# A two-block network on one core: decay rows of the state-space part by DMA, head pairs in column halves, group products in PSUM, differences on GpSimd

## What is computed

```python
def _ssd(xh, dt, a, bm, cm):                  # 32 heads of 64, 4 groups of 8 heads, state 128
    x = (xh * dt[..., None])...
    a_cs = jnp.cumsum(dt * a, axis=2)
    seg = a_cs[:, :, :, None] - a_cs[:, :, None, :]
    lmat = jnp.exp(jnp.where(causal, seg, -jnp.inf))
    cb = jnp.einsum('bclgn,bcsgn->bclsg', cc, bc)
    y_diag = jnp.einsum('bclsgr,bcsgrp->bclgrp', cb[..., None] * lmat, x)
    ...                                       # plus what earlier chunks pass on
y = _ssd(xh, dt, a, bm, cm) + d_skip[:, None] * xh
```

## Time and profile before

| what | value |
|---|---|
| median of 3 runs | 3531.86 us (3529.06 to 3532.5) |
| the profiled execution, own time | 3530.74 us |
| its span | 3529.1 us |
| PE busy | 2966.5 us, 84% of the span |
| DVE, ACT, POOL busy | 892.6, 701.1 and 153.8 us |
| bytes read from memory | 567.76 MB |
| chain that ended last, by engine | PE 69%, DMA 22%, DVE 3%, ACT 3% |

### The profile page before, as it was taken

The page is one execution under the profiler, slowest core; times in us unless marked ns, Lnnn a source line. Parts: engine busy times, 40 slices in busy tenths (PEclk is TensorE's granted clock), DMA queues, the critical chain, the costliest instruction groups (busy, mean ns, idle before and its releaser), DMA issues.

```text
span 3529.1 us, 39001 instructions
## 1 busy us (share of the span) xinstructions
PE 2966.5 (84%) x14533; PEld 1462.5 (41%) x14534; DVE 892.6 (25%) x1741; ACT 701.1 (20%) x1221; POOL 153.8 (4%) x262
## 2 busy tenths in 40 slices
PE   5999999999984766666666664998899999988999
PEld 3445544344434222222222222554654436455444
DVE  1335659800122000000000003311440114025211
ACT  2113301200111111111111111213641012155310
POOL 1000000000000000000000000000130000002100
PEclk9999999999995989888888887999999999998999
DMA  7251012222223899999999993222002122200020
GB/s 196 96 187 52 1 48 72 71 72 72 72 74 148 333 425 425 424 424 424 424 425 425 424 390 122 70 86 72 1 1 71 48 97 98 79 28 1 25 81 38
DMA packets 125332, 584.16 MB, mean 166 GB/s; under 512 B 15844, under 2 KB 26692, under 8 KB 100660
## 3 DMA queue, kind: packets, MB, share of 16 engines
q1 hardware_dynamic: 107232, 558.06, 39.6%
q0 software_dynamic: 12080, 17.36, 1.9%
q10 hardware_dynamic: 5924, 7.41, 0.6%
HBM read 567.76 MB, written 14.94 MB: 165 GB/s over the span
## 4 chain that ended last, share of the span: by engine, by line
PE 69%; DMA 22%; DVE 3%; ACT 3%; issue 1%; SPq 0%; ACTq 0%; POOL 0%; DVEq 0%; POOLq 0%
PE PS L1508 63%; DMA S<-in_w 19%; PE PS L727 4%; PE PS L935 1%; DMA S<-in_x 1%; DMA ring<-in_w_in 1%; DMA S<-sorted_rows 1%; ACT TAIL L1123 0%; ACT TAIL L1121 0%; ACT TAIL L1119 0%; SPq L293 0%; DVE RSTD L1952 0%; DVE S L2106 0%; ACT L1130 0%; PE PS L395 0%
## 5 line engine op out<-in xcount | busy, mean ns | idle before, releaser
L1508 PE MATMUL PS<-nT,ring 128*128 128x512 f32 x2432 | 1071.5, 600 | 25.0 <-DVE nT L1956 10.3
L1508 PEld LDWEIGHTS PS<-nT,ring 128*128 128x128 f32 x2432 | 466.4, 193 | 608.5 <-issue 597.5
L1508 PE MATMUL PS<-S 128*32 128x256 f32 (+5 forms) x3344 | 366.9, 549 | 137.5 <-DMA S<-in_w 116.4
L1508 PE MATMUL PS<-ring,S 128*32 128x256 f32 (+1 forms) x3360 | 335.9, 555 | 164.3 <-DMA ring<-in_w 137.5
L1508 PE MATMUL PS<-S,ring 128*128 128x512 f32 x896 | 386.2, 592 | 2.5 <-DVE S L1392 1.7
L1508 PEld LDWEIGHTS PS<-ring,S 128*32 128x32 f32 x3360 | 133.4, 127 | 332.8 <-issue 318.4
L1508 PEld LDWEIGHTS PS<-S 128*32 128x32 f32 (+2 forms) x3344 | 138.1, 133 | 315.7 <-issue 268.9
L1508 PEld LDWEIGHTS PS<-S,ring 128*128 128x128 f32 x896 | 170.0, 190 | 216.6 <-issue 216.6
L570 DVE TENSOR_TENSOR S<-S,PS 128x128 f32<-128x128 f32 x65 | 18.7, 287 | 720.6 <-ACT S L487 720.6
L2106 DVE SCALAR_TENSOR_TENSOR S<-S,COL 128x512 f32<-128x512 f32 x240 | 161.0, 744 | 0.1
L487 ACT ACTIVATE S<-PS 128x128 f32<-128x128 f32 x65 | 18.0, 277 | 544.2 <-PE PS L1508 544.2
(11 more groups left out here) (325 smaller groups left out, 2297.6 us busy)
## 6 DMA issues: line engine op xcount, KB each, us to landing
ring<-in_w SPq DMA_DIRECT2D x96, 2048.0 KB, 21.5
S<-in_w SPq DMA_DIRECT2D x96, 2048.0 KB, 21.6
ring<-in_w_in SPq DMA_DIRECT2D x40, 2048.0 KB, 7.8
ring<-in_w_ada SPq DMA_DIRECT2D x12, 2048.0 KB, 11.9
expert_rows<-S POOLq DMA_DIRECT2D x65, 128.0 KB, 10.4
ring<-in_w_ssm_out SPq DMA_DIRECT2D x4, 2048.0 KB, 7.7
ring<-in_cmp_w SPq DMA_DIRECT2D x4, 2048.0 KB, 8.3
ring<-in_w_out SPq DMA_DIRECT2D x4, 2048.0 KB, 7.9
```

Source lines behind the costliest of these rows:

```text
L1508: return pe.matmul(o, l, r, start=start, stop=stop)
```

## The change

- The rows of `RR` are written once to a tensor in device memory (`decay_rows`, 32 x 1280) by a DMA on GpSimd's queue. SyncE then issues one DMA per head that reads one row of it and writes it to all 128 partitions of a buffer of `EB`: 5 KB read 128 times, 640 KB written.
- `EB` has five buffers in place of two, where `CB` and part of `RR` were. The row of head h may be issued once the pair that used its buffer is through on PE: rows 2c+5 and 2c+6 once pair c is.
- GpSimd takes the four differences per head, in place, SBUF to SBUF; ACT's exponentials read and write the same buffer.
- The masked product of a group stays in PSUM (banks 0 to 2 or 3 to 5, in turn by group), masked there by DVE; ACT's copy goes. `masked` multiplies a buffer of `EB` by PSUM.
- PE has no `head_rows`. `pair_y` does two heads in one go and alternates between the halves of the output partitions.
- SyncE's DMAs for heads 0 and 1 stand behind the load of slab GL0, those for heads 2 to 31 between the loads of GL0+2 and GL0+3.

```diff
@@ sync @@
+            def decay_rows(heads):
+                for h in heads:
+                    if h >= NEB:
+                        sp.wait_ge(S("y_mm"), 2 * ((h - NEB) // 2 + 1))
+                    elif h >= 2:
+                        sp.wait_ge(S("xbc_done"), KX)
+                    else:
+                        sp.wait_ge(S("rr_stored"), 16)
+                    sp.dma_start(EB[:, head_buffer(h), :], rr_d[h:h + 1, :].to_broadcast([P, PACK])) \
+                        .then_inc(S(f"row{head_buffer(h)}_landed"), 16)
...
+                if i == GL0 + 1:
+                    decay_rows(range(2))
+                if i == GL0 + NSLOT:
+                    decay_rows(range(2, HEADS))
@@ gpsimd @@
+            pool.wait_ge(S("scalar_milestone"), AFTER["cums_copied"] + 2)
+            pool.dma_start(rr_d, RR[0:HEADS, :]).then_inc(S("rr_stored"), 16)
+            for h in range(HEADS):
+                row_landed(pool, h)
+                for i in range(NT):
+                    pool.tensor_scalar(EB[:, head_buffer(h), P * i:P * i + P], EB[:, head_buffer(h), P * i:P * i + P],
+                                       LS[:, 32 * i + h:32 * i + h + 1], 0.0, ALU.subtract, ALU.min) \
+                        .then_inc(S("diag_exponent"), 1)
@@ tensor @@
+            def pair_y(c):
+                pe.wait_ge(S("m_ready"), 2 * c + 2)
+                if c >= 2:
+                    pe.wait_ge(S("y_out"), c - 1)
                 for i in range(NT):
-                    x_ = XD[:, i, HD * h:HD * h + HD]
-                    m = mm(o[:, P * i:P * i + P], x_, E_[:, P * i:P * i + P], i == 0, i == NT - 1)
+                    for e in range(2):
+                        h = 2 * c + e
+                        o = PS[64 * e:64 * e + 64, 6 + c % 2, :]
+                        m = mm(o[:, P * i:P * i + P], XD[:, i, HD * h:HD * h + HD],
+                               EB[:, head_buffer(h), P * i:P * i + P], i == 0, i == NT - 1)
...
+            group_cb(0)
+            group_cb(1)
+            for c in range(KI):
+                pair_y(c)
+                if c % 4 == 3 and c < 8:
+                    group_cb(c // 4 + 2)
@@ scalar @@
+                row_landed(act, h)
                 for i in (0, 2, 1):
...
+                act.wait_ge(S("diag_exponent"), NT * (h + 1))
+                act.activation(E_[:, 0:512], E_[:, 0:512], ACT.Exp).then_inc(S("e_ready"), 1)
@@ vector @@
+                dve.tensor_tensor(E_, E_, PSF[:, b:b + PACK], ALU.mult).then_inc(S("m_ready"), 1)
```

More of the change, by code:

```diff
@@ L128, in build @@
         S2, S3 = TAIL[:, 0:4096], TAIL[:, 4096:8192]
-        CB, RR = TAIL[:, 8192:9472], TAIL[:, 9472:10752]
+        RR = TAIL[:, 9472:10752]
         X0 = v3(S0[:, 0:4096], D)
@@ L138, in build, with head_buffer @@
         BC = v3(S2, T)
-        EB = v3(TAIL[:, 4096:4096 + 2 * PACK], PACK)
+        NEB = 5
+        EB = v3(TAIL[:, 4096:4096 + NEB * PACK], PACK)
+        def head_buffer(h):
+            return (h + 3) % NEB
         ZS = v3(TAIL[:, 0:1024], T)
@@ L219, in build @@
         sorted_d = nc.dram_tensor("sorted_rows", [NASG, D], F32).ap()
+        rr_d = nc.dram_tensor("decay_rows", [HEADS, PACK], F32).ap()
         y_d = nc.dram_tensor("expert_rows", [NASG + WIN, D], F32).ap()
@@ L1433, in dve_second, with row_landed @@
                 dve.tensor_copy(OUTB[:, n // 2, 512 * (n % 2):512 * (n % 2) + 512], PS[:, n % 4, :]).then_inc(S("out_rows"), 1)
+        def row_landed(eng, h):
+            eng.wait_ge(S(f"row{head_buffer(h)}_landed"), 16 * (h // NEB + 1))
         block = ctx.enter_context(nc.Block())
@@ L1618, in _, with group_cb @@
             ada_columns(11, 2 * 512 + 4 * (11 - ADA0))
-            def group_cb(g, r):
+            def group_cb(g):
                 pe.wait_ge(S("xbc_done"), KX)
-                if r >= 2:
-                    pe.wait_ge(S("rb_dve"), r - 1)
-                    pe.wait_ge(S("rb_act"), r - 1)
+                if g >= 2:
+                    pe.wait_ge(S("m_ready"), HPG * (g - 1))
                 else:
@@ L1636, in group_cb @@
                                BC[:, 4 + g, P * (i + 1):T], True, True)
[L1637 to L1655, removed]
-                for i in range(NT):
-                    x_ = XD[:, i, HD * h:HD * h + HD]
-                    m = mm(o[:, P * i:P * i + P], x_, E_[:, P * i:P * i + P], i == 0, i == NT - 1)
-                    if i in OFF:
-                        m = mm(o[:, P * (i + 1):T], x_, E_[:, OFF[i]:OFF[i] + OFFW[i]], False, False)
-                m.then_inc(S("y_mm"), 1)
@@ L1663, in _ @@
-            pe.wait_ge(S("scalar_milestone"), AFTER["cums_copied"] + 2)
[L1664 to L1677, removed]
+                m.then_inc(S("cb_product"), 1)
@@ new lines, in pair_y @@
+            def pair_y(c):
+                pe.wait_ge(S("m_ready"), 2 * c + 2)
+                if c >= 2:
+                    pe.wait_ge(S("y_out"), c - 1)
+                for i in range(NT):
+                    for e in range(2):
[3 more added lines that the diff above has]
+                               EB[:, head_buffer(h), P * i:P * i + P], i == 0, i == NT - 1)
+                        if i == NT - 1:
+                            m.then_inc(S("y_mm"), 1)
+                    for e in range(2) if i in OFF else ():
+                        h = 2 * c + e
+                        mm(PS[64 * e:64 * e + 64, 6 + c % 2, P * (i + 1):T], XD[:, i, HD * h:HD * h + HD],
+                           EB[:, head_buffer(h), OFF[i]:OFF[i] + OFFW[i]], False, False)
@@ L1678, in _ @@
+            pe.wait_ge(S("scalar_milestone"), AFTER["cums_copied"] + 2)
+            group_cb(0)
[4 more added lines that the diff above has]
+                    group_cb(c // 4 + 2)
+            pe.wait_ge(S("m_ready"), HEADS)
             pe.wait_ge(S("y_out"), KI)
@@ L1864, in _ @@
                         .then_inc(S("xbc_done"), 1)
-            r = 0
             for h in range(HEADS):
[L1868 to L1882, removed]
-                for i in (0, 2, 1):
[L1884 to L1889, removed]
+                E_ = EB[:, head_buffer(h), :]
+                row_landed(act, h)
+                for i in (0, 2, 1):
+                    act.activation(E_[:, OFF[i]:OFF[i] + OFFW[i]], E_[:, OFF[i]:OFF[i] + OFFW[i]], ACT.Exp,
+                                   bias=LS[:, P + 32 * i + h:P + 32 * i + h + 1]).then_inc(S("off_exp"), 1)
+                act.wait_ge(S("diag_exponent"), NT * (h + 1))
+                act.activation(E_[:, 0:512], E_[:, 0:512], ACT.Exp).then_inc(S("e_ready"), 1)
             for n in range(KD):
@@ L2024, in _, with group_masked @@
             gain(32, C_N2)
+            def group_masked(g):
+                b = 1536 * (g % 2)
+                dve.wait_ge(S("cb_product"), g + 1)
+                dve.tensor_tensor(v3(PSF[:, b:b + 512], P), v3(PSF[:, b:b + 512], P),
+                                  tri[:, None, 0:P].to_broadcast([P, NT, P]), ALU.mult).then_inc(S("cb_ready"), 1)
             def masked(h):
+                g, E_ = h // HPG, EB[:, head_buffer(h), :]
+                b = 1536 * (g % 2)
+                dve.wait_ge(S("cb_ready"), g + 1)
+                dve.wait_ge(S("off_exp"), 3 * h + 3)
                 dve.wait_ge(S("e_ready"), h + 1)
-                dve.tensor_tensor(EB[:, h % 2, :], EB[:, h % 2, :], CB[:, :], ALU.mult).then_inc(S("m_ready"), 1)
+                dve.tensor_tensor(E_, E_, PSF[:, b:b + PACK], ALU.mult).then_inc(S("m_ready"), 1)
             def y_pair(c):
@@ L2034, in y_pair @@
                                          in1=PS[:, 6 + c % 2, :], op0=ALU.mult, op1=ALU.add).then_inc(S("y_out"), 1)
-            r = 0
+            group_masked(0)
+            group_masked(1)
             for h in range(HEADS):
[L2038 to L2060, removed]
+                masked(h)
+                if h % 2 and h >= 3:
                     y_pair(h // 2 - 1)
-            masked(HEADS - 1)
+                if h in (9, 17):
+                    group_masked(h // HPG + 1)
             y_pair(KI - 1)
```

2 lines of the change are left out of this document (1 added, 1 removed).

## The result

| | before | after |
|---|---|---|
| median of 4 runs, us | 3530.46 (3527.97 to 3532.50) | 3489.53 (3487.67 to 3493.31) |
| profiled execution, us | 3530.74 | 3489.33, span 3487.7 |
| first matmul of the GLU projection, us | 449.84 | 409.99 |

The ratio is 0.9886, 95% interval 0.9869 to 0.9903. The time lies 8.5 us above the forecast of 3481 and inside its range. In the profiled executions the GLU projection starts 39.85 us sooner, and another 1.6 us come from the stages behind it.

What follows compares the result with a forecast made beforehand. PE bounds the stage before; after, a five-buffer loop, 8.3 us plus a 4.6 us pair, 12.9 a turn. Pair 1 ending at 309.0, seven turns and 1.0 us give GLU start 400.3, 49.5 us sooner: 3481 us, range 3462 to 3506.

Steps and rivals of the forecast that it cites:

- What bounds before, and what is removed: Stage before the GLU projection: PE sets its time at 4.65 us a head; the change removes 2.34 us of that.
- Two halves side by side: PE's y matmuls: two heads in alternating output halves run together, 2.5 us a pair at full clock, against 4.65 in turn.
- Rival (c): PE's pairs: halves don't run side by side, 3482 us; second form, weight loads stand in the way, 3491; chance 0.06, both.
- The loop through five buffers: Stage after: row landing, GpSimd, ACT, DVE, PE pair and buffer release form a loop, 12.9 us a turn of two pairs.
- Landing, 4.2 us: DMA of one 640 KB row into a buffer: 4.2 us a turn, taken from the positions broadcast and a slab.
- rival (d): Row DMAs: rows come slowly, 8.9 us each, 3655 us, slower than before; chance 0.04 with other ways to slower.
- The pair at the low clock, 4.6: First pair of a turn on PE: runs at 1.2 GHz after an idle stretch, streaming doubled, 4.6 us.
- Rival (a): PE's pairs in the loop: clock stays full, pair 2.5 us, turn 10.8 us, time 3464; chance 0.17.
- GpSimd, 4 x 0.44 = 1.76 us: GpSimd's four differences per head in the loop: 1.76 us, from two 128-column instructions taking 0.88 us.
- Rival (b): Loop links dearer: differences 0.775 us each, 3493 us; or row landing 6 us, 3494; both 3506; chance 0.18.
- Opening: Stage start: rows wait behind two slabs, row 3 lands at 300.0, pair 1 ends at 309.0 us.
- Engines at once: DVE's mask beside GpSimd's differences: one PSUM operand avoids contention; product in SBUF would add up to 1.49 us per turn.

Runs made afterwards that it cites:

- the serial kernel: Changed kernel with all seven matmuls of a pair's even head before the odd head's, no alternation between output halves; 3500.68 us (one run).
- the filled kernel: Changed kernel with nine extra 256-column matmuls on PE, results unused, behind every even pair but the last; 3484.51 us, ratio to before 0.9865.
- the forms kernel: Changed kernel with six forms of tensor_scalar on 128x128, four of each, run first on GpSimd beside an idle DVE; 3491.33 us (one run).

## Why the prediction was right, and where it missed

The profiled execution came out at 3489.33 against 3481, 8.3 us more. At the GLU start the miss is 9.7 us (409.99 against 400.3). By its steps:

**What bounds before, and what is removed: right.** Two halves side by side: 2.39 us a pair against 2.5 taken from the earlier trace rows, and 4.17 in series. The Trainium skill (TensorE: Matmul & The Clock Gate, Part 3, Packing small matmuls) has weight loads overlap only across row groups. The trace of after disagrees, as that of before did: 28 matmuls and 28 loads of one row group, 1.65 us of loads, in 2.39 us. The prediction read that section one-sidedly: it also gives a speedup of 2.38 for three column tiles, and with that the trace agrees in kind, with 1.75 for two halves. Rival (c) is out in both forms, and with the serial kernel so is the idea that side by side would not matter: it is worth 13.8 us at the GLU start.

**The loop through five buffers: right.** The chain of after is that loop, link by link. Four buffers lengthen the turn to 16.5 us, eight dissolve it.

**Landing, 4.2 us: right.** The seven on the chain are 3.75 to 4.51, mean 4.14. The value from the broadcast of positions and the slab was the one to take; rival (d) is out.

**The pair at the low clock, 4.6: right in kind, a little high.** The seven on the chain have a mean of 4.32 us, 3.92 to 4.53, at a granted 0.50 to 0.70. Where a pair ran wholly low it took 4.5, 2.1 us more than at full clock, which is the 2.13 us of streaming that the sum doubled. Rival (a), the clock holding, is refuted; the filled kernel shows that the rival's mechanism exists once something fills the gaps.

**GpSimd, 4 x 0.44 = 1.76 us: the step that failed.** It is 4 x 0.69 = 2.79. The 0.88 us of the earlier trace rows for two of 128 columns was the nearest row in width, but it was a multiplication by two scalars. Rival (b) took 0.775 from the 512-column instructions of the same rows; on the real form it is nearly right, by luck of the number: it is the price of 512 columns of multiplications, and what the forms kernel found is a dearer pair of operations on 128. In seven turns this is 7.2 us, read off the chain of after; the rest of the turn is 1.8 us under the sum, mostly the pair.

**Opening: right in place, 4.3 us short.** Pair 1 ended at 313.34 and not at 309.0. Of this, 1.7 us is the projection, which ended later in this execution; the row on the chain, row 2, then landed 0.9 us sooner than the sum had row 3 (300.79 against 300.0 + 1.7). The other 3.5 us lie on GpSimd: 5.64 us from the landing to the last difference, where the sum had 2.1. It had put row 2's differences ahead of row 3's landing. In fact both rows' eight differences came in one piece behind the landing of row 2. At 0.44 us each these eight would have taken 3.5 us and not 5.55, so 2.0 of the 3.5 us are the price again, and 1.5 the order of landings and differences that the sum had wrong.

Together: 1.7 - 0.9 + 3.5 + 7.2 - 1.8 = 9.7 us. The price of GpSimd's differences is 9.2 of it (7.2 + 2.0); the errors of the other terms, 1.8 us at most, have both signs and nearly cancel, and that part of the nearness is luck. The experiment with the differences on DVE hit its time by two misses that cancel, 3.4 us more from the opening and 4.5 us less from the turns.

**Engines at once.** The Trainium skill (SBUF — State Buffer, Who interferes with whom) lets a DVE instruction with one input in PSUM run free of a GpSimd one. Here the trace agrees: beside the masks a difference takes 13.82 / 20 = 0.69 us, the same as in the forms kernel beside an idle DVE. Heads 0 and 1 show the other case. The four differences of head 0 met an idle DVE, 2.81 us for four; those of head 1 lie beside DVE's convolution, of which three instructions in five read two inputs from SBUF, and took 3.75 us. Timeline of GpSimd in after, and windows around the two heads:

```profile
300.87 13.82 POOL L1529 TENSOR_SCALAR TAIL<-TAIL,LS 128x128 f32<-128x128 f32 x20 [24.48 <-DMA TAIL<-decay_rows]
```

```profile
269.74:272.55 2.81, 2.81 (x7) 1.15 (x7) 0.00 (x0) 0.22 (x1) 2.80 (x4) 1.00 0.25 91
272.64:276.39 3.75, 3.75 (x10) 1.63 (x9) 3.32 (x5) 0.90 (x2) 3.75 (x4) 1.00 0.00 0
```

So beside two inputs in SBUF a difference takes 0.94 us in place of 0.70, a third more on average, and four still went through while DVE was busy for 3.32 us. The kernel with the product left in SBUF was not run.

## What to carry to other kernels

When work leaves the engine that bounds a stage, draw the loop that takes its place (which buffer frees which load, and who stands in between) and count a turn; here five buffers in place of eight cost some 19 us, and leaving all differences on GpSimd another 22. Price each link from a row with the same operations, not only the same width: one wrong row on GpSimd was nearly the whole miss. And before giving up PE's bound, ask what the clock does in the gaps it will have: here a pair went from 2.39 to 4.3 us on the path that counts.

## What the runs showed of the hardware

- On GpSimd the pair of operations sets the price of a tensor-scalar instruction: 0.35 to 0.44 us for two multiplications over 128x128 f32, 0.69 to 0.78 for subtract and min, multiply and min, or subtract and add.
- A GpSimd difference of 0.70 us beside an idle DVE took 0.94 us on average beside DVE's convolution, which reads two inputs from SBUF, and 0.69 beside its masks, which read one.
- Alternating column halves gave 1.75 times the rate of the same matmuls in series (2.39 and 4.17 us a pair at full clock).
- One row of device memory spread over 128 partitions, 640 KB, landed 3.75 to 4.51 us after its issue where it stood first behind a pair and no slab was in flight, as the estimate from other loads had it (4.2). Over all 32 rows of after, slabs and rows in flight included, the median is 5.3 us.
- Useless matmuls between the pairs made the stage 7 us shorter, since the granted clock stayed up (0.90 over the stage against 0.77).
